# A gated group norm's scaling cut into two parts of two tiles, a weight tile apart

## The chip, the cores and the metric

The kernel runs on one core of one Trainium2 chip. The metric is the device time of one execution in microseconds (us). The kernel before took 1035.56 us (median of 3 runs, 1034.97 to 1035.7).

## The reference

Three transformer-like layers on 256 tokens of width 1024, in fp32. Layers 0 and 1 are a retention layer and a differential-attention layer, each with memory attention and a feed-forward part. Layer 2, which the change touches, has two mixers side by side, a state-space one (ssd, 16 heads) and a forgetting attention (fox, 16 heads). The end of the state-space mixer is a gated norm over two groups of 512 features:

```python
yg = (y * jax.nn.silu(z.astype(jnp.float32))).reshape(b, s, SSD_GROUPS, SSD_WIDTH // SSD_GROUPS)
yg = yg * lax.rsqrt(jnp.mean(yg * yg, axis=-1, keepdims=True) + NORM_EPS)
return (yg.reshape(b, s, SSD_WIDTH) * norm_w.astype(jnp.float32)).astype(xbc_raw.dtype)
```

Both mixers' outputs are then multiplied by the output weights and added to the stream x.

## The kernel before

Every large product runs with fp32 operands split into a high and a low part, three matmuls for each pair of 128x128 blocks. Weights stream through a ring of four slots. For each weight tile SyncE issues the load, ScalarE (ACT) copies the high part (`split_hi`, L1259), VectorE (DVE) subtracts to get the low part (`split_lo`, L1781), and TensorE (PE) multiplies (`project`). ACT and DVE split the tile that is four ahead of the one whose slot it takes. Two PSUM banks alternate in the input projection.

Layer 2's input projection `in2` has 45 weight tiles (slots 0 to 44); the first output projection `oa2` follows it (slots 45 to 52) and takes the eight state-space tiles as inputs, in order 0 to 7. Between the weight tiles the engines do the small work of the mixers. `plans()` writes by hand which step stands in which slot; each engine goes through the same list in program order and runs the steps that it has a part in, so an engine that waits in one step holds back all that stands behind it on that engine.

- PE runs the steps of a slot after that weight tile, except that `spread` and `ssd_out` come halfway through the next weight tile. From slot 20 on, tiles are taken in pairs with tokens on the partitions; the even slot's end completes a pair.
- DVE runs a slot in this order: early steps (`ssd_weights`, `norm_out`, then `ssd_skip` or `fox_probs`), the evacuation of the product (only even slots from 22 on), middle steps (`group_out`), `split_lo`, then late steps (`norm`, `ssd_gate`, `fox_values`, `fox_scores`, `head_sums`).
- ACT runs `split_hi`, then the slot's steps in plan order.
- GpSimd (POOL) runs its steps in plan order, without weight tiles: `ssd_mask` (L1729), `fox_bias` (L1738), `ssd_square` (L1721), `mix` (L1712).

The step of the change: `group_norm` (slot 29 for group 0, slot 40 for group 1) has PE form the mean of squares in bank 4 and ACT a first inverse root. `group_out` (slots 30 and 41) has DVE refine the root in three instructions (L1992, L1994, L2045) and scale the four 128x256 tiles of the group (L2049). The last one raises `np_out`. Then `mix` (slots 31 and 42) has ACT copy the high part of each of the four tiles (L1507) and POOL subtract to get the low part (L1712); `oa2` needs both (`mix_lo`).

`np_out` counts finished norms in order and has more readers. PE's `heads_turn` (the `spread` of the query and key norms, L1009) waits until all norms issued before it are out, since they use bank 4. ACT's `squares` (L1411) of norm n waits for norm n-2, whose buffer it takes over; the norm two behind group 0 is that of tiles 30 and 31 (`squares`, 30 in slot 31):

```python
if n >= 2:
    act.wait_ge(np_out, n - 1)
```

Around the change the plan has these steps (a selection). Slot 30: `group_out` 0, `ssd_square` 4, `ssd_weights` 5, `norm` 22. Slot 31: `ssd_skip` 5, `squares` 30, `spread` 22, `ssd_gate` 5, `ssd_decay` 12 and 13 (L1540), `fox_values` 0 (ACT L1563, then DVE L2202), `fox_scores` 1 (DVE L2189, then ACT L1550), `head_sums` 30, `mix` 0 to 3. Slot 32: `norm_out` 22 (L2031), `fox_probs` 1 (L2198, L1558), `ssd_square` 5, `ssd_out` 6 (L1189), `ssd_weights` 6 (L2164), `norm` 30, `fox_bias` 2. Slot 33: `ssd_skip` 6 (L2179), `spread` 30, `ssd_gate` 6 (L2209), `ssd_decay` 14 and 15, `fox_weights` 1 (L1106). Slot 34: `norm_out` 30, `ssd_weights` 7, `fox_scores` 2 (PE L1097). Slot 41: `group_out` 1, `fox_probs` 4, `head_sums` 26. Slot 42: `norm` 26, `mix` 4 to 7. Slot 43: `squares` 34, `spread` 26, `fox_values` 4, `fox_scores` 5. Slot 44: `norm_out` 26, `fox_probs` 5, `norm` 34, `fox_bias` 6. Slot 45: `spread` 34, `fox_weights` 5.

Of the kernel before, what the change touches and what calls it, by code (L numbers as in the profile page):

```python
# [24 lines left out]
T = 256  # L25
# [165 lines left out]
def plans():  # L191


    plan = {0: [[] for _ in range(28)], 1: [[] for _ in range(28)], 2: [[] for _ in range(61)]}

    def at(layer, slot, kind, *key):
        plan[layer][slot].append((kind, *key))
# [78 lines left out]
    for h, slots in enumerate(((9, 10, 11, 12), (11, 12, 13, 14), (13, 14, 15, 18), (15, 16, 17, 19),  # L276
                               (18, 19, 20, 21), (20, 21, 22, 23))):
        first, soft, turned, last = slots
# [44 lines left out]
    for j in range(4):  # L323
# [7 lines left out]
        for n in range(2):  # L331
            p, slot = 2 * j + n, a + 7 + 3 * n
# [6 lines left out]
        plan[2][21 + 2 * p].insert(0, ("ssd_skip", p))  # L339
    for g, slot in ((0, 29), (1, 40)):  # L340
        at(2, slot, "group_norm", g)
        plan[2][slot + 1].insert(0, ("group_out", g))
        for k in range(4):
            at(2, slot + 2, "mix", 4 * g + k)
    return plan


def program(nc, x_in, mem_in, params_in, consts_in, w, small_rows, out):
    f32, f32r = mybir.dt.float32, mybir.dt.float32r
    ALU, ACT = mybir.AluOpType, mybir.ActivationFunctionType  # L350
    AX = mybir.AxisListType.X
    PH, WIDTH = phases()
    PLAN = plans()
    NRING = len(WIDTH)
    MUL, ADD, SUB = ALU.mult, ALU.add, ALU.subtract
    ds = bass.ds

    with ExitStack() as ctx:
# [3 lines left out]
        def sem(name):  # L362
            return ctx.enter_context(nc.semaphore(name))
# [35 lines left out]
        def normed(n):  # L399
            return roots_b[:, :] if n % 2 else tmp[:, 1024:1536]  # L400
# [63 lines left out]
        np_sq, np_ms, np_ln, np_rt, np_nt, np_out = (sem(f"norm_{s}") for s in ("sq", "ms", "ln", "rt", "nt", "out"))  # L464
# [34 lines left out]
        def tile(buf, k, width=T):  # L499
            return buf[:, ds(k * T, width)]  # L500
# [4 lines left out]
        def pcol(name, k=0, rows=P):  # L505
            return par[0:rows, ds(k + PCOL[name], 1)]
# [19 lines left out]
        def eps(which, rows=P):  # L526
            return par[0:rows, PCOL["eps"] + which:PCOL["eps"] + which + 1]
# [60 lines left out]
        for layer in range(3):  # L588
            for steps in PLAN[layer]:
                for kind, *key in steps:  # L590
                    k = (layer, *key)
# [28 lines left out]
        def norm_bank(n):  # L620

            first = min(number["norm", k] for _, k in number if type(k[0]) is str and k[1] == 1 and _ == "norm")
            count_ = sum(1 for _, k in number if type(k[0]) is str and k[1] == 1 and _ == "norm")
            return bank[7 if 0 <= n - first < count_ and (n - first) % 2 else 4]
# [1141 lines left out]
        def _(dve):  # L1766
            V = nc.vector
# [219 lines left out]
            def newton_step(n, y, v=None):  # L1987


                dve.wait_ge(np_rt, n + 1)  # L1990
                v = norm_bank(n)[:, 0:y.shape[1]] if v is None else v
                V.scalar_tensor_tensor(v, v, eps(0), y, ADD, MUL).then_inc(np_nt, 1)  # L1992
                dve.wait_ge(np_nt, 5 * n + 1)
                V.tensor_tensor(v, v, y, MUL).then_inc(np_nt, 1)  # L1994
                dve.wait_ge(np_nt, 5 * n + 2)
                return v
# [41 lines left out]
                                                  norm_bank(norm_no(layer, t))[:, :], MUL, MUL)  # L2038
                last.then_inc(np_out, 1)

            def group_out(layer, g):
                n = number["norm", ("group_norm", layer, g)]
                y = normed(n)[:, 0:T]
                v = newton_step(n, y)
                V.scalar_tensor_tensor(y, v, -3.0, y, ADD, MUL).then_inc(np_nt, 3)  # L2045
                dve.wait_ge(np_nt, 5 * n + 5)
                for t in range(4 * g, 4 * g + 4):
                    y = tile(u, 8 + t)
                    last = V.scalar_tensor_tensor(y, y, pcol("ssdn", t), normed(n)[:, 0:T], MUL, MUL)  # L2049
                last.then_inc(np_out, 1)  # L2050

            def ret_scores(layer, h):
                dve.wait_ge(r_s, h + 1)
# [151 lines left out]
            def ssd_gate(layer, t):  # L2205
# [3 lines left out]
                V.tensor_tensor(y, y, tile(u, t), MUL).then_inc(ss_g, 1)  # L2209

            DO = {"head_sums": head_sums, "norm": norm, "norm_out": norm_out, "norm_soon": norm_out, "group_out": group_out, "ret_scores": ret_scores, "gated": gated, "gated_early": gated, "scores": scores,
                  "maxima_mid": scores, "softmax_mid": softmax, "norm_mid": norm_out, "mix_low": mix_low,
                  "mix_low_early": mix_low,
# [52 lines left out]
            for s in range(2):  # L2266
                last = V.tensor_tensor(lam[0:64, s:s + 1], par[0:64, lc + 2 * s:lc + 2 * s + 1],
                                       par[0:64, lc + 2 * s + 1:lc + 2 * s + 2], MUL)
# [134 lines left out]
```

## Time and profile before

| what | value |
|---|---|
| median of 3 runs | 1035.56 us |
| the profiled execution's own time | 1035.94 us |
| its span in the trace | 1034.0 us |
| TensorE busy | 1015.1 us, 98% |
| VectorE busy | 804.1 us, 78% |
| ScalarE busy | 635.6 us, 61% |
| GpSimd busy | 265.7 us, 26% |
| mean granted TensorE clock | 0.998 |

The span is the time from the first to the last instruction in the trace; the execution's own time holds 1.94 us more around it. The granted clock is a share of 2.4 GHz, so 0.50 is the lower level, 1.2 GHz. In the trace's rows an instruction has a start, a duration, its engine, its line in the kernel, what it writes and reads, and in brackets how long its engine stood idle before it and for whom.

### The profile page before, as it was taken

Reading aid. Unit: us, or ns where it says so; the run is one execution under the profiler, and the core shown is the slowest. Engines: PE = TensorE matmul, PEld = TensorE weight load, DVE = VectorE, ACT = ScalarE, POOL = GpSimd, SP = SyncE. Lnnn points to the kernel's source line nnn. Section 1 sums busy time; section 2 is a strip of 40 time slices with the busy share of each in tenths; the row PEclk is TensorE's granted clock in tenths of the full one; section 3 lists DMA queues with packets and bytes.
Section 4 is the critical chain, followed back from the end, with each engine's and each line's share of the span. In section 5 each row is a group of like instructions: output and inputs, shape, how many; then the busy total and the mean of one; then the engine's idle time right before and its main releaser. Section 6 shows DMA issues by size and latency. Waiting matters only on the chain.

```text
span 1034.0 us, 21367 instructions
## 1 busy us (share of the span) xinstructions
PE 1015.1 (98%) x7196; PEld 926.9 (90%) x7196; DVE 804.1 (78%) x1360; ACT 635.6 (61%) x1183; POOL 265.7 (26%) x236
## 2 busy tenths in 40 slices
PE   8999999999999999999999999999899999999998
PEld 7999988888889898888888899998798899999988
DVE  6875897877665988987787658979978689998843
ACT  7653786656554666765666446766776666666532
POOL 3200044544110000244453110035321034444300
PEclk9999999999999999999999999999999999999999
DMA  8543465565655332656555664565344455555663
GB/s 303 184 135 100 124 223 195 182 193 182 200 179 193 128 107 64 202 185 197 186 183 179 199 201 154 169 204 190 132 159 134 151 171 184 183 183 183 186 199 103
DMA packets 56898, 178.61 MB, mean 173 GB/s; under 512 B 6240, under 2 KB 11648, under 8 KB 56704
## 3 DMA queue, kind: packets, MB, share of 16 engines
q1 hardware_dynamic: 56832, 177.73, 53.5%
q8 instruction: 41, 0.67, 0.3%
q14 instruction: 25, 0.20, 0.1%
HBM read 176.63 MB, written 1.08 MB: 172 GB/s over the span
## 4 chain that ended last, share of the span: by engine, by line
PE 52%; DVE 6%; ACT 3%; issue 1%; DMA 1%; DVEq 0%; SPq 0%; ACTq 0%
PE bank L822 7%; PE bank L820 5%; PE bank L821 5%; PE bank L818 4%; PE bank L816 4%; PE scores L822 4%; PE scores L816 4%; PE scores L818 4%; PE scores L820 2%; PE scores L821 2%; PE bank L815 2%; PE scores L815 2%; DVE ring_parts L1781 1%; PE bank L848 1%; PE bank L849 1%
## 5 line engine op out<-in xcount | busy, mean ns | idle before, releaser
L1781 DVE TENSOR_TENSOR ring_parts<-ring_raw,ring_parts 128x1024 fp32r<-128x1024 f32 (+2 forms) x343 | 423.1, 1236 | 34.4 <-ACT ring_parts L1259 28.8
L1259 ACT ACTIVATE ring_parts<-ring_raw 128x1024 fp32r<-128x1024 f32 (+2 forms) x343 | 340.9, 997 | 73.9 <-PE scores L816 31.1
L822 PE MATMUL bank<-xw_parts,ring_parts 128*128 128x256 f32 x648 | 182.3, 281 | 0.0
L820 PE MATMUL bank<-xw_parts,ring_parts 128*128 128x256 f32 x472 | 136.4, 289 | 0.2 <-DVE con L1932 0.2
L821 PE MATMUL bank<-xw_parts,ring_parts 128*128 128x256 f32 x472 | 133.5, 283 | 0.0
L822 PEld LDWEIGHTS bank<-xw_parts,ring_parts 128*128 128x128 f32 x648 | 123.4, 190 | 7.5
L848 PE MATMUL bank<-ring_parts,xw_parts 128*128 128x256 f32 x384 | 114.3, 298 | 0.2 <-DVE u L1975 0.2
L849 PE MATMUL bank<-ring_parts,xw_parts 128*128 128x256 f32 x384 | 108.9, 284 | 0.0
L850 PE MATMUL bank<-ring_parts,xw_parts 128*128 128x256 f32 x384 | 108.9, 284 | 0.0
L1679 POOL TENSOR_TENSOR act_parts<-tmp,act_parts 128x256 f32 (+1 forms) x66 | 61.6, 933 | 166.4 <-ACT act_parts L1335 166.4
L822 PE MATMUL scores<-xw_parts,ring_parts 128*128 128x256 f32 x352 | 98.6, 280 | 0.0
L822 PE MATMUL bank<-act_parts,ring_parts 128*128 128x256 f32 x337 | 94.5, 281 | 0.0
L820 PEld LDWEIGHTS bank<-xw_parts,ring_parts 128*128 128x128 f32 x472 | 90.3, 191 | 2.2 <-issue 1.3
L821 PEld LDWEIGHTS bank<-xw_parts,ring_parts 128*128 128x128 f32 x472 | 90.4, 191 | 0.1
L848 PEld LDWEIGHTS bank<-ring_parts,xw_parts 128*128 128x128 f32 x384 | 73.7, 192 | 7.4 <-issue 6.9
L1675 POOL TENSOR_TENSOR scratch<-scratch 128x256 f32<-128x256 f32 x47 | 46.5, 989 | 119.6 <-ACT scratch L1270 118.2
L1687 POOL TENSOR_TENSOR tmp<-tmp,rstd 128x256 f32<-128x256 f32 x44 | 74.1, 1684 | 9.4 <-ACT tmp L1340 9.2
L849 PEld LDWEIGHTS bank<-ring_parts,xw_parts 128*128 128x128 f32 x384 | 73.8, 192 | 0.1
L850 PEld LDWEIGHTS bank<-ring_parts,xw_parts 128*128 128x128 f32 x384 | 73.7, 192 | 0.0
L822 PEld LDWEIGHTS scores<-xw_parts,ring_parts 128*128 128x128 f32 x352 | 66.9, 190 | 7.5
L1340 ACT ACTIVATE tmp<-tmp 128x256 f32<-128x256 f32 x66 | 27.6, 419 | 70.7 <-DVE tmp L1941 41.9
L818 PE MATMUL scores<-xw_parts,ring_parts 128*128 128x512 f32 x176 | 70.0, 398 | 0.5 <-DVE xw_parts L1787 0.5
(267 smaller groups left out, 2594.3 us busy)
## 6 DMA issues: line engine op xcount, KB each, us to landing
ring_raw<-w_up SPq DMA_DIRECT2D x132, 512.0 KB, 3.5
ring_raw<-w_in SPq DMA_DIRECT2D x85, 512.0 KB, 3.6
ring_raw<-w_down SPq DMA_DIRECT2D x48, 512.0 KB, 3.7
ring_raw<-w_down SPq DMA_DIRECT2D x24, 384.0 KB, 4.0
ring_raw<-w_oa SPq DMA_DIRECT2D x16, 256.0 KB, 2.6
ring_raw<-w_ob SPq DMA_DIRECT2D x16, 256.0 KB, 2.9
ring_raw<-w_oa SPq DMA_DIRECT2D x8, 512.0 KB, 3.5
ring_raw<-w_ob SPq DMA_DIRECT2D x8, 512.0 KB, 3.6
```

Of the source, the lines that this page charges most:

```text
L816: return mm(ps[:, 0:2 * T], w_hi, tile(parts, 2 * t, 2 * T), start=False, stop=stop)
L818: mm(ps[:, 0:2 * T], w_hi, tile(parts, 2 * t, 2 * T), start=start, stop=False)
L820: mm(ps[:, 0:T], w_hi, high(parts, t), start=start, stop=False)
L821: mm(ps[:, 0:T], w_hi, low(parts, t), start=False, stop=False)
L822: return mm(ps[:, 0:T], w_lo, high(parts, t), start=False, stop=stop)
L848: mm(o, x_hi, w_hi, start=not second and k == 0 and tt == 0, stop=False)
L849: mm(o, x_hi, w_lo, start=False, stop=False)
L850: last = mm(o, x_lo, w_hi, start=False, stop=second and k == 3 and tt == 1)
L1259: A(ring_hi[:, slot * DM:slot * DM + width], ring_raw[:, slot * DM:slot * DM + width], ACT.Copy).then_inc(hi_done, 1)
L1679: G.tensor_tensor(low(act_parts, f), two(prod, h), high(act_parts, f).bitcast(f32), SUB).then_inc(ffn_lo, 1)
L1687: G.tensor_tensor(two(gate_s, h), two(gate_s, h), rstd[:, :], MUL).then_inc(silu_scaled, 1)
L1781: V.tensor_tensor(ring_lo[:, a:b], ring_raw[:, a:b], ring_hi[:, a:b].bitcast(f32), SUB).then_inc(lo_done, 1)
```

## The change

`group_out` gets a third key, the part. Part 0 (slots 30 and 41) refines the root and scales the first two tiles; part 1 (slots 31 and 42) scales the other two and raises `np_out`. The four `mix` steps of each group move from slots 31 and 42 to slots 32 and 43, at the end of each slot's list.

```diff
@@ plans()
     for g, slot in ((0, 29), (1, 40)):
         at(2, slot, "group_norm", g)
-        plan[2][slot + 1].insert(0, ("group_out", g))
+        for part in range(2):
+            plan[2][slot + 1 + part].insert(0, ("group_out", g, part))
         for k in range(4):
-            at(2, slot + 2, "mix", 4 * g + k)
+            at(2, slot + 3, "mix", 4 * g + k)
     return plan
@@ vector engine
-            def group_out(layer, g):
+            def group_out(layer, g, part):
+
                 n = number["norm", ("group_norm", layer, g)]
-                y = normed(n)[:, 0:T]
-                v = newton_step(n, y)
-                V.scalar_tensor_tensor(y, v, -3.0, y, ADD, MUL).then_inc(np_nt, 3)
-                dve.wait_ge(np_nt, 5 * n + 5)
-                for t in range(4 * g, 4 * g + 4):
+                if part == 0:
+                    y = normed(n)[:, 0:T]
+                    v = newton_step(n, y)
+                    V.scalar_tensor_tensor(y, v, -3.0, y, ADD, MUL).then_inc(np_nt, 3)
+                    dve.wait_ge(np_nt, 5 * n + 5)
+                for t in range(4 * g + 2 * part, 4 * g + 2 * part + 2):
                     y = tile(u, 8 + t)
                     last = V.scalar_tensor_tensor(y, y, pcol("ssdn", t), normed(n)[:, 0:T], MUL, MUL)
-                last.then_inc(np_out, 1)
+                if part:
+                    last.then_inc(np_out, 1)
```

## Rows read from the trace of the kernel before

**Rows 1.** The page's busy time of each engine: time, share of the span, instructions
```profile
PE 1015.1 (98%) x7196; PEld 926.9 (90%) x7196; DVE 804.1 (78%) x1360; ACT 635.6 (61%) x1183; POOL 265.7 (26%) x236
```
**Rows 2.** Stretches, us: busy time (instructions) of PE, PEld, DVE, ACT, POOL; PEclk; DMA
```profile
739.40:743.00 3.60, 3.60 (x20) 3.60 (x19) 3.07 (x3) 3.57 (x10) 3.60 (x5) 0.53 0.24 61
...
790.00:800.00 10.00, 8.64 (x60) 6.78 (x59) 8.85 (x19) 6.38 (x16) 0.00 (x0) 1.00 0.42 145
```
**Rows 3.** PE's waits, 690 to 800 us: total, times, longest
```profile
PE bank L1189 <- DVE tmp L2164: 1.9, 1, 1.9
PE scores L1097 <- DVE u L2031: 1.8, 2, 1.3
PE bank L1009 <- DVE u L2013: 1.4, 3, 0.6
PE scores L1106 <- ACT tmp L1558: 1.4, 1, 1.4
```
**Rows 4.** DVE's timeline, slots 30 to 32: start, duration, instruction, idle before it
```profile
727.44 2.64 DVE L2049 SCALAR_TENSOR_TENSOR u<-u,par,tmp 128x256 f32<-128x256 f32 x4
730.00 1.21 DVE L1781 TENSOR_TENSOR ring_parts<-ring_raw,ring_parts 128x1024 fp32r<-128x1024 f32 x1
...
732.86 1.22 DVE L1781 TENSOR_TENSOR ring_parts<-ring_raw,ring_parts 128x1024 fp32r<-128x1024 f32 x1
...
734.33 0.42 DVE L2202 TENSOR_TENSOR act_parts<-bank,act_parts 128x256 fp32r<-128x256 f32 x1
...
737.03 0.95 DVE L2164 TENSOR_TENSOR tmp<-tmp,u 128x768 f32<-128x768 f32 x1
...
739.40 1.63 DVE L1781 TENSOR_TENSOR ring_parts<-ring_raw,ring_parts 128x1024 fp32r<-128x1024 f32 x1 [0.76 <-ACT ring_parts L1259]
741.52 0.81 DVE L1992 SCALAR_TENSOR_TENSOR heads<-heads,par 128x8 f32<-128x8 f32 x1 [0.49 <-ACT heads L1416]
```
**Rows 5.** ACT's timeline, slots 31 and 32
```profile
730.17 0.63 ACT L1411 ACTIVATE tmp<-u 128x512 f32<-128x512 f32 x1 [1.57 <-DVE u L2049]
730.71 1.48 ACT L1540 ACTIVATE tmp<-tmp 128x256 f32<-128x256 f32 x4
732.10 0.36 ACT L1563 ACTIVATE act_parts<-bank 128x256 fp32r<-128x256 f32 x1
...
737.10 1.32 ACT L1507 ACTIVATE act_parts<-u 128x256 fp32r<-128x256 f32 x4
```
**Rows 6.** PE's timeline, slots 31 to 34
```profile
732.61 0.66 PE L1009 MATMUL bank<-con,u 128*128 128x128 f32 x4
...
738.03 0.87 PE L1189 MATMUL bank<-tmp,x_tok 128*64 128x256 f32 x8 [1.91 <-DVE tmp L2164]
...
744.59 0.66 PE L1009 MATMUL bank<-con,u 128*128 128x128 f32 x4 [0.41 <-DVE u L2013]
...
747.98 0.38 PE L1097 MATMUL scores<-u 64*128 64x128 f32 x2 [0.50 <-DVE u L2031]
```
**Rows 7.** POOL's mixes: timeline, then the line L1712's min, median, max in ns
```profile
737.58 4.04 POOL L1712 TENSOR_TENSOR act_parts<-u,act_parts 128x256 fp32r<-128x256 f32 x4 [8.18 <-ACT act_parts L1507]
L1712 POOL TENSOR_TENSOR act_parts<-u,act_parts x8: 722/730/1704, 737.6 to 785.4; 128x256 fp32r<-128x256 f32 x8
```
**Rows 8.** DVE's small norm step L1992: count, min, median, max ns
```profile
L1992 DVE SCALAR_TENSOR_TENSOR heads<-heads,par x8: 215/228/809, 702.5 to 793.4; 128x8 f32<-128x8 f32 x8
```
**Rows 9.** Timelines of DVE, ACT and PE around slots 42 to 45
```profile
783.40 0.69 DVE L1992 SCALAR_TENSOR_TENSOR heads<-heads,par 128x8 f32<-128x8 f32 x1
...
788.75 0.40 ACT L1550 ACTIVATE tmp<-tmp,negmax 128x128 f32<-128x128 f32 x1 [3.46 <-DVE negmax L2189]
...
786.75 0.66 PE L1009 MATMUL bank<-con,u 128*128 128x128 f32 x4 [0.56 <-DVE u L2013]
788.67 0.40 PE L818 MATMUL bank<-act_parts,ring_parts 128*128 128x512 f32 x1
...
793.00 0.88 PE L1106 MATMUL scores<-con,tmp 128*128 128x128 f32 x6 [1.35 <-ACT tmp L1558]
```

## The prediction

> **What bounds the kernel now.** I read the page's busy times first: PE is busy for 1015.1 us of a span of 1034.0 [rows 1]. So nothing that this change does can matter unless it moves one of PE's idle spells or the clock that PE gets. The work of PE is not changed. Next I read PE's waits in the stretch that the change touches, slots 23 to 48, 690 to 800 us [rows 3]. There are seven, together 6.5 us: one on `ssd_weights` (1.9), two on `norm_out` (1.8), three on the token-wise norms (1.4), one on ACT's attention weights (1.4). All but the last are on DVE. Of them the change can reach five: 1.91 us at 738.03, 0.41 at 744.59, 0.50 at 747.98 [rows 6], 0.56 at 786.75 and 1.35 at 793.00 [rows 9], sum 4.7. Then the clock: in 739.40 to 743.00 PE was granted 0.53 of full speed, so nearly all the time at the lower level, 1.2 GHz [rows 2]. What PE did before that was to stand idle for 1.91 us. The dip costs (1 - 0.53) x 3.6 = 1.7 us. So 4.7 + 1.7 = 6.4 us is all that the change could win here, were every wait gone.
>
> Between 727 and 738 DVE has work at almost every moment, and PE waits for the end of that queue: the row of `ssd_weights` 6 starts at 737.03, and PE's `ssd_out` 6 at 738.03 [rows 4, 6]. `group_out` lies in that queue.
>
> **Group 0, part 0 (slot 30).** The change takes two of four L2049 out of slot 30. The four took 2.64 us from 727.44 [rows 4], so 0.66 each. But they are put back in slot 31 ahead of `split_lo`, and between the two places DVE waits for nobody: the split at 730.00, the norm of 22, `ssd_skip` 5 and the split at 732.86 follow each other at once. So the whole of `group_out` is now over where the split of slot 31 starts today, at about 732.9 instead of 730.1, and everything from that split on starts when it did. Gain on DVE's queue: nothing. The split and the norm between are some 0.8 to 1.3 us earlier, and nobody waits for them except PE's L1009 at 732.61 [rows 6], which from now on has to wait for `np_out` (bank 4) as well, until about 732.9. That puts PE's arrival at `ssd_out` 6 off by 0.3 us, and it would find the queue not finished anyway. Cost nothing here.
>
> **Group 0, the wait of ACT (slot 31).** This is the term that I think is real. ACT's `squares` 30 takes over the group norm's buffer and waits for `np_out`; it stood idle 1.57 us for L2049 already and began at 730.17 [rows 5]. It can now begin at about 732.95, 2.8 us later. Queued behind it on ACT are `ssd_decay` 12 and 13 (1.48) and the copy of `fox_values` 0, which began at 732.10 and ended at 732.46, 2.3 us after the squares began [rows 5]. So that copy ends at 732.95 + 2.3 = 735.25. DVE wants it for L2202, at 734.33 [rows 4]. DVE stalls 735.3 - 734.33 = 0.95 us, and `fox_scores` 1, `head_sums` 30, `norm_out` 22 and `ssd_weights` 6 behind it are late by as much. `ssd_out` 6 starts at 739.0 instead of 738.03, and PE's idle spell is 1.91 + 0.95 - 0.3 = about 2.6 us. **+0.95 us** on PE's time at that point. The clock falls as before; I take the dip at its present 1.7 us.
>
> **Group 0, the mixes (slot 31 to 32).** The four L1507 took 1.32 us of ACT ahead of `split_hi` of slot 32 [rows 5], and DVE's split at 739.40 had waited 0.76 us for that one [rows 4]. With ACT's exponentials 0.95 us late and the mixes gone from there, `split_hi` comes at 738.2 to 739.2, and DVE, which reaches its split at 739.6, doesn't wait. The norm of 30 (741.52, after a wait of 0.49 for ACT [rows 4]) comes 0.2 us earlier. So DVE has made good its delay there. Then the mixes come, behind the norm on ACT at about 741.3 to 742.6, ahead of `split_hi` of slot 33, and on POOL behind `ssd_square` 5 and `fox_bias` 2, at about 743 to 747. Today POOL's four mixes take 737.58 to 741.62 [rows 7], where DVE has idle gaps. While POOL works, DVE's instructions with both inputs in SBUF are stretched: the split at 739.40 took 1.63 against 1.21, L1992 0.81 against a median of 0.228 [rows 4, 8], and one mix took 1.704 against 0.730 [rows 7]. In the new place DVE has the norm's multiply, a split, `ssd_gate` 6 and `ssd_weights` 7. I bound what that adds before `norm_out` 30, for which PE waits at 747.98 [rows 6]: below, nothing (the stretching only moves); above, four times the 0.42 us of the split, 1.7 us, less the 0.2 that DVE is ahead, so +1.5. I take 0.7, since POOL's total is the same and only the place is worse.
>
> The Trainium skill, "SBUF — State Buffer", section "SBUF: two separate sides", says that a GpSimd instruction and a DVE instruction with two SBUF inputs lock each other out for the whole of an instruction. By it each of the four mixes could hold up one DVE instruction for its whole 0.73 us, at most 2.9 us in all, and then PE's time after 748 would be about 2.2 us later than mine; the trace agrees that such instructions alternate, in the stretched rows of [rows 4, 7, 8], though less than whole lengths were lost.
>
> **Sum of group 0 at 748 us.** PE is 0.95 late at 738. The waits of 0.41 and 0.50 [rows 6] absorb 0.91 of it, if DVE is on time for them; DVE is 0 to 1.5 late, 0.5 with my value (0.7 - 0.2). PE leaves 747.98 at +0.5; bounds 0.05 and 1.5. After it PE has no wait until 786, so that stays.
>
> **Group 1.** Two L2049 leave slot 41 and come back in slot 42, before its split. `norm` 26 starts at 783.40 as before, but POOL is now silent, so its three small instructions take about 0.2 each instead of 0.69 [rows 8, 9], 1.4 less, and I put another 0.4 on L2013. PE's wait of 0.56 at 786.75 goes: **-0.56**. DVE is then 1.8 us ahead, and ACT's exponentials of `fox_scores` 5 start at 788.75 - 1.8 = 786.9 [rows 9]. Behind them come the mixes (slot 43), ACT 788.7 to 790.0, POOL from 789.1. At 0.73 each without contention, the low parts of tiles 4 to 7 are there at 789.85, 790.6, 791.3 and 792.0; with one of them 1.7 long, the last at 793.0. Here is what is late next: `oa2` began at 788.67 and was through its first tile 1.35 before 793.00, at 791.65 [rows 9], 0.37 us for each of eight blocks. It now begins at 788.1, so it wants input 4 at 789.6 and input 7 at 790.7. It will stand idle at every one of them and end at 792.4 to 793.4, not 791.1. Behind it PE's L1106 started at 793.00 after a wait of 1.35 for ACT [rows 9]; ACT would be ready at 792.4. So PE starts L1106 at 792.4 to 793.4 against 793.00: **-0.6 to +0.4**, I take 0 (the middle, rounded toward contention). The wait of 1.35 is replaced by the wait for the mixes.
>
> **The sum** against the profiled execution's own 1035.94 us: +0.5 + 0 = 1036.4. That execution was 0.38 above the median of the runs, so against the median it is 1035.56 + 0.5 = **1036.1 us**. A measurement of this kernel can tell about 0.2%, 2.1 us, from no change, so this is "no change".
>
> **Rivals.** (a) POOL against DVE decides: the mixes of group 0 stretch all four DVE instructions, the bound of +1.5 comes true and group 1 ends at +0.4: +1.9, **1037.5 us**. For it: [rows 8]; against it: it only decides if POOL's mixes fall fully between 743 and 747. It is still within the 0.2%. (b) Slower: the clock falls a second time. Its place is `oa2`'s first tile, 789.5 to 793.4, where PE would idle 1.5 to 2.5 us in pieces; its price is the measured 1.7 us of the first dip, on top of +0.5 and +0.4: +2.6, **1038.2 us**. It decides once PE's idle share there is that of 736 to 738, where 1.91 us was followed by a fall; 1.35 us at 791.6 was not, PEclk is 1.00 in 790 to 800 [rows 2, 6, 9]. The same price falls due if the longer idle spell at 738 prolongs the dip. (c) Faster: the ACT wait is absorbed and DVE gets through earlier, because its small norm steps no longer collide with POOL (3 x 0.5 us in each group). Then the waits at 738 (to below 1.5 us), 744.59, 747.98 and 786.75 shrink by 0.5 + 0.41 + 0.50 + 0.56 = 2.0, and without the long idle spell the clock stays up: -1.7. Together -3.7, **1031.9 us**. Against it: `squares` 30 waits for the last L2049 [rows 5], and no DVE work before 737 becomes less. (d) The change does nothing, since the two parts lie in the same unbroken DVE queue and all waits only trade places: 0, 1035.6. It is one end of my own case.
>
> **How the numbers follow.** My case with (d) at its lower end: 0.60. (a) 0.18. (b) 0.13. (c) 0.09. Within 0.2%: 0.60 + 0.18 = 0.78, and a little of (b) and (c) falls short of the limit, so 0.80; slower 0.12; faster 0.08. The range takes in the bounds of my case (-0.6 to +1.9), half a us of spread between runs, and part of (b): 1034.5 to 1038.1.
>
> **What would show it.** In the profile after: L1411 with a longer idle before it (about 4.3 us, 1.57 before), L2202 in slot 31 with an idle near 0.95 for ACT's L1563, PE's L1189 with 2.6 instead of 1.91. No idle before the split of slot 32. The wait at 786.75 gone. PE idle on POOL's L1712 before four products of `oa2`. A PEclk near 0.5 only once, after 739. I am wrong if L2202 has no wait, if the clock doesn't dip after 738, or if it dips near 793 as well.

## The result, and the profile after

The changed kernel took 1037.44 us, the kernel before, timed beside it, 1035.70 us (medians of 19 runs each). The ratio is 1.0017, 95% interval 1.0011 to 1.0023: slower by 1.7 us, within the 0.2% that the prediction called "no change", but clear of zero. The profiled execution took 1037.02 us, with a span of 1035.1.

PE's waits from 690 to 800 us, as in [rows 3]: total, times, longest.

```profile
PE bank L1190 <- DVE tmp L2168: 2.5, 1, 2.5
PE scores L1098 <- DVE u L2032: 2.5, 2, 1.3
PE bank L816 <- POOL act_parts L1713: 1.1, 1, 1.1
PE bank L1010 <- DVE u L2052: 0.6, 1, 0.6
PE bank L1010 <- DVE u L2014: 0.4, 1, 0.4
PE bank L819 <- POOL act_parts L1713: 0.4, 1, 0.4
```

Lines have moved: most by 1, `ssd_weights` from L2164 to L2168, the norm's scaling L2049 to L2052. Three waits are new, of two kinds: one for the last L2052 (bank 4), two for POOL's mixes. The wait for ACT's attention weights before L1106 is gone.

All of the loss arises between three starts on PE that every trace has: `fox_scores` 1 (716.56 before, 716.29 after), `fox_scores` 2 (747.98 and 748.83), and `fox_weights` 5 (793.00 and 794.27). The first stretch went from 31.42 to 32.54 us, **+1.12**; the second from 45.02 to 45.44, **+0.42**. Together +1.54, against +1.7 in the medians (the two profiled executions are only 1.08 apart, since the changed one was 0.27 ahead at 716 us and 0.2 quicker after the second stretch). I use these two stretches for every kernel below, since what happens before 716 us differs from execution to execution by several tenths. A stretch comes from one trace. In traces of programs that are the same up to there it repeats within 0.1 us (31.36 to 31.47, 32.53 to 32.63), with one exception of 0.23 that is explained below.

First stretch, ACT in slot 31, then DVE in slots 31 to 34 (as [rows 5] and [rows 4]):

```profile
732.83 0.63 ACT L1412 ACTIVATE tmp<-u 128x512 f32<-128x512 f32 x1 [4.49 <-DVE u L2052]
733.36 1.48 ACT L1541 ACTIVATE tmp<-tmp 128x256 f32<-128x256 f32 x4
734.75 0.36 ACT L1564 ACTIVATE act_parts<-bank 128x256 fp32r<-128x256 f32 x1
```

```profile
732.65 1.22 DVE L1782 TENSOR_TENSOR ring_parts<-ring_raw,ring_parts 128x1024 fp32r<-128x1024 f32 x1
...
735.15 0.42 DVE L2206 TENSOR_TENSOR act_parts<-bank,act_parts 128x256 fp32r<-128x256 f32 x1 [0.94 <-ACT act_parts L1564]
...
739.38 1.22 DVE L1782 TENSOR_TENSOR ring_parts<-ring_raw,ring_parts 128x1024 fp32r<-128x1024 f32 x1
741.18 0.36 DVE L1993 SCALAR_TENSOR_TENSOR heads<-heads,par 128x8 f32<-128x8 f32 x1 [0.59 <-ACT heads L1417]
...
743.03 1.11 DVE L2014 TENSOR_TENSOR u<-u,heads 128x512 f32<-128x512 f32 x1
744.07 0.47 DVE L2183 SCALAR_TENSOR_TENSOR u<-u,par,bank 128x256 f32<-128x256 f32 x1
744.46 1.36 DVE L1782 TENSOR_TENSOR ring_parts<-ring_raw,ring_parts 128x1024 fp32r<-128x1024 f32 x1
745.75 0.95 DVE L2213 TENSOR_TENSOR u<-u 128x256 f32<-128x256 f32 x1
746.63 1.48 DVE L2168 TENSOR_TENSOR con<-con,u 128x768 f32<-128x768 f32 x1
748.03 0.74 DVE L2032 TENSOR_SCALAR u<-bank,par 128x512 f32<-128x512 f32 x1
```

ACT stood idle for 4.49 us where it had 1.57, and passed it on to DVE as an idle of 0.94 in front of L2206. The split at 739.38 now waits for nobody (0.76 before). But the next lines are stretched: L2014 1.11 against 0.69 without POOL, the split 1.36 against 1.22, L2213 0.95 against 0.42, L2168 1.48 against 0.95. Sum 1.62 us. Counted from `fox_scores` 1 in both kernels, DVE is 1.09 us late at L2168 (`ssd_weights` 6). When L2014 starts, at 743.03, it has made that good and is 0.54 ahead (L2013 started at 743.84 before). At L2032 it is 1.12 late (L2031, 747.18 before), and that is the whole loss of the stretch. The trace of the kernel before has the same multiply once beside POOL's mixes of group 1, and as long:

```profile
785.58 1.12 DVE L2013 TENSOR_TENSOR u<-u,heads 128x512 f32<-128x512 f32 x1
```

POOL's rows in the changed kernel say why; the second is group 1:

```profile
742.86 4.44 POOL L1713 TENSOR_TENSOR act_parts<-u,act_parts 128x256 fp32r<-128x256 f32 x4
...
789.98 3.78 POOL L1713 TENSOR_TENSOR act_parts<-u,act_parts 128x256 fp32r<-128x256 f32 x4 [14.17 <-ACT act_parts L1508]
```

PE's rows over both stretches (as [rows 6, 9]):

```profile
732.88 0.63 PE L1010 MATMUL bank<-con,u 128*128 128x128 f32 x4 [0.55 <-DVE u L2052]
...
738.86 0.87 PE L1190 MATMUL bank<-tmp,x_tok 128*64 128x256 f32 x8 [2.48 <-DVE tmp L2168]
...
748.83 0.93 PE L1098 MATMUL scores<-u 64*128 64x128 f32 x8 [1.17 <-DVE u L2032]
...
790.76 0.50 PE L819 MATMUL bank<-act_parts,ring_parts 128*128 128x512 f32 x1 [0.44 <-POOL act_parts L1713]
...
793.81 0.39 PE L816 MATMUL bank<-act_parts,ring_parts 128*128 128x256 f32 x1 [1.05 <-POOL act_parts L1713]
...
794.27 0.81 PE L1107 MATMUL scores<-con,tmp 128*128 128x128 f32 x6
```

And the clock, the last but two of the columns, here 0.66 and 1.00: one fall, after 738, none at the first output tile.

```profile
740.00:745.00 5.00, 5.00 (x32) 5.00 (x31) 4.24 (x7) 4.97 (x16) 4.20 (x6) 0.66 0.29 105
790.00:795.00 5.00, 3.36 (x17) 2.01 (x17) 3.07 (x5) 4.71 (x12) 5.00 (x6) 1.00 0.17 51
```

### The profile page after: what moved, and what is told of

Read it like the earlier page. It is cut to its first block, busy times and chain, and to the rows that moved or that the text cites. A ratio compares the mean times of both kernels' runs of the same rounds, so it can differ in the third digit from the quotient of the medians.

```text
span 1035.1 us, 21367 instructions
## 1 busy us (share of the span) xinstructions
PE 1016.6 (98%) x7196; PEld 928.3 (90%) x7196; DVE 804.0 (78%) x1360; ACT 635.7 (61%) x1183; POOL 265.9 (26%) x236
## 3 DMA queue, kind: packets, MB, share of 16 engines
HBM read 176.63 MB, written 1.08 MB: 172 GB/s over the span
## 4 chain that ended last, share of the span: by engine, by line
PE 52%; DVE 6%; ACT 3%; issue 1%; POOL 0%; DVEq 0%; ACTq 0%
PE bank L823 7%; PE bank L821 5%; PE bank L822 5%; PE bank L819 4%; PE bank L817 4%; PE scores L823 4%; PE scores L819 4%; PE scores L817 4%; PE scores L821 2%; PE scores L822 2%; PE bank L816 2%; PE scores L816 2%; DVE ring_parts L1782 2%; PE bank L849 1%; PE bank L850 1%
## 5 line engine op out<-in xcount | busy, mean ns | idle before, releaser
L819 PE MATMUL bank<-xw_parts,ring_parts 128*128 128x512 f32 x176 | 69.7, 396 | 0.8 <-DVE xw_parts L1788 0.8
```

The source lines that it names most:

```text
L819: mm(ps[:, 0:2 * T], w_hi, tile(parts, 2 * t, 2 * T), start=start, stop=False)
```

## The experiments

All experiments are in this table, but for two more profiles of the kernel with the mixes moved alone, which come at the end. "Stretch 1" is from PE's `fox_scores` 1 to 2, "stretch 2" on to `fox_weights` 5, from one trace; the ratios are to the kernel before, timed beside it (medians of 11 runs, before of 27 to 33). A ratio is estimated together with its interval and can differ from the quotient of the two medians by up to 0.0005. An interval is about 0.9 us to either side, so the medians tell apart only the largest differences, and most of what follows rests on the stretches.

| kernel | stretch 1 | stretch 2 | median us | before | ratio, interval |
|---|---|---|---|---|---|
| before | 31.42 | 45.02 | | | |
| changed (19 runs) | 32.54 | 45.44 | 1037.44 | 1035.70 | 1.0017 (1.0011 to 1.0023) |
| mixes moved alone | 31.42 | 45.44 | 1037.58 | 1035.86 | 1.0016 (1.0007 to 1.0025) |
| split alone | 32.30 | 45.03 | 1036.64 | 1035.86 | 1.0008 (0.9999 to 1.0017) |
| group 0 alone | 32.53 | 45.00 | 1037.29 | 1035.86 | 1.0015 (1.0006 to 1.0024) |
| group 1 alone | 31.19 | 45.41 | 1036.59 | 1035.86 | 1.0012 (1.0003 to 1.0022) |
| changed, squares behind | 31.51 | 46.92 | 1036.71 | 1035.92 | 1.0012 (1.0002 to 1.0021) |
| changed, mixes 0 late | 31.29 | 45.43 | 1036.71 | 1035.92 | 1.0005 (0.9996 to 1.0014) |
| changed, mixes 1 first | 32.63 | 45.03 | 1036.86 | 1035.92 | 1.0009 (1.0000 to 1.0018) |
| before, mixes 0 late | 30.19 | 45.03 | 1034.74 | 1035.92 | 0.9987 (0.9978 to 0.9996) |
| the same, weights first | 29.86 | 45.03 | 1034.46 | 1035.92 | 0.9986 (0.9977 to 0.9995) |
| changed, all three mended | 29.88 | 45.02 | 1034.30 | 1035.92 | 0.9986 (0.9977 to 0.9995) |

**Which half of the change costs?** Mixes moved, `group_out` whole:

```diff
-            at(2, slot + 2, "mix", 4 * g + k)
+            at(2, slot + 3, "mix", 4 * g + k)
```

> Only the mix steps move a slot later; group_out stays whole. Theory (two terms: ACT's squares of 30 wait 2.8 us longer because of the split, and POOL's mixes stretch VectorE's instructions in a worse place): without the split, PE's idle spell before ssd_out 6 stays at 1.9 us, the squares' idle stays near 1.6, but the mixes still hit VectorE in slots 33 and 34, so PE's wait before scores 2 is about 1.2 to 2 us against 0.5, and group 1 ends 0.4 us late: +1.0 to +1.5 us over the kernel before. Rival (the split makes the whole loss): 0 to +0.3 us.

Stretch 1 is 31.42, exactly as before: in group 0 the new place is no worse than the old one. The part of the theory that gave it +0.6 to +1.1 fell. Stretch 2 is +0.42, as expected. DVE's rows show how the zero comes about:

```profile
737.85 1.21 DVE L1781 TENSOR_TENSOR ring_parts<-ring_raw,ring_parts 128x1024 fp32r<-128x1024 f32 x1
739.65 0.37 DVE L1992 SCALAR_TENSOR_TENSOR heads<-heads,par 128x8 f32<-128x8 f32 x1 [0.59 <-ACT heads L1416]
...
741.50 1.11 DVE L2013 TENSOR_TENSOR u<-u,heads 128x512 f32<-128x512 f32 x1
```

The idle of 0.76 before the split is gone, the split is 0.42 shorter and L1992 0.44 (1.63 and 0.81 in [rows 4]), together 1.62. The four instructions from L2013 on are stretched by as much again. The median doesn't follow the stretches: it is +1.7 us, as much as for the whole change and 1.3 more than they explain. The profiled execution was this kernel's fastest, at 1035.36 us. I come back to that.

**The split alone**, on the changed kernel:

```diff
-            at(2, slot + 3, "mix", 4 * g + k)
+            at(2, slot + 2, "mix", 4 * g + k)
```

> Only the split of group_out; the mixes stay in slots 31 and 42. Theory: squares of 30 idle 4.5 us, PE idle 2.5 us before ssd_out 6, but no mixes in slots 33 and 34, so about 0 to +0.9 us from group 0, and group 1 near 0: +0.3 to +0.9 us. Rival (the mixes' place is the whole loss): 0. Rival (the split makes the whole loss): +1.7 us.

Stretch 1 is +0.88, stretch 2 unchanged, the median +0.8, within what the theory had. DVE in that trace:

```profile
735.92 0.42 DVE L2206 TENSOR_TENSOR act_parts<-bank,act_parts 128x256 fp32r<-128x256 f32 x1 [0.94 <-ACT act_parts L1564]
...
740.99 1.63 DVE L1782 TENSOR_TENSOR ring_parts<-ring_raw,ring_parts 128x1024 fp32r<-128x1024 f32 x1 [0.76 <-ACT ring_parts L1260]
...
746.20 1.21 DVE L1782 TENSOR_TENSOR ring_parts<-ring_raw,ring_parts 128x1024 fp32r<-128x1024 f32 x1
```

The 0.94 us is there, the old idle of 0.76 and the old stretched split of 1.63 too. So 0.94 of delay comes in, and 0.88 arrives at `fox_scores` 2: with the mixes in their old place DVE makes up next to nothing.

**One group at a time.** The key `part` and the moved mixes for one group only; the other has both parts in one slot and its mixes where they were:

```diff
-        for part in range(2):
-            plan[2][slot + 1 + part].insert(0, ("group_out", g, part))
+        for part in (0, 1) if g == 0 else (1, 0):
+            plan[2][slot + 1 + (part if g == 0 else 0)].insert(0, ("group_out", g, part))
-            at(2, slot + 3, "mix", 4 * g + k)
+            at(2, slot + (3 if g == 0 else 2), "mix", 4 * g + k)
```

> The whole change for group 0 only. Theory: +1.1 us, all of it there by PE's scores 2 near 749 us; the stretch after 780 us as in the kernel before. Rival (group 1's mixes, late for the output projection, make most of the loss): under +0.4 us.

+1.11 in stretch 1 and nothing in stretch 2, as the theory had it; the median is +1.4.

The same with `g == 1`:

> The whole change for group 1 only. Theory: PE's wait before the norm transposes at 786.8 (0.56 us) goes, waits of together 1.5 us for POOL's mixes come in the first tile of the output projection, the wait of 1.35 us for ACT goes: +0.4 us in sum. Rival (group 1 makes most): +1.2 us or more.

+0.39 in stretch 2 (45.41). The wait of 1.35 for ACT is gone, POOL's 0.44 and 1.05 are there. By the ratios group 1 seems to cost as much as group 0, but the intervals overlap widely; of its 11 runs seven lie between 1035.87 and 1036.65, four between 1037.49 and 1038.66. I come back to that.

This kernel's stretch 1 is that of the kernel before in its program, and its trace shows something about the clock. First the stretches 730 to 750, then PE's rows:

```profile
730.00:740.00 10.00, 8.10 (x69) 6.87 (x66) 9.07 (x24) 6.71 (x21) 2.19 (x3) 1.00 0.41 132
740.00:750.00 10.00, 7.97 (x67) 6.72 (x65) 9.20 (x13) 6.93 (x17) 4.41 (x6) 1.00 0.42 133
```

```profile
738.26 0.87 PE L1190 MATMUL bank<-tmp,x_tok 128*64 128x256 f32 x8 [1.90 <-DVE tmp L2168]
741.04 0.87 PE L1107 MATMUL scores<-con,tmp 128*128 128x128 f32 x6 [0.28 <-ACT tmp L1559]
744.59 0.66 PE L1010 MATMUL bank<-con,u 128*128 128x128 f32 x4 [1.24 <-DVE u L2014]
747.98 0.93 PE L1098 MATMUL scores<-u 64*128 64x128 f32 x8 [0.51 <-DVE u L2032]
```

The idle spell is the same 1.90 us, and the clock did not fall. Yet stretch 1 is only 0.23 us shorter. From `ssd_out` 6 to `fox_scores` 2 PE's own time was 1.35 us shorter than in the kernel before, and its waits were 1.12 longer: 0.28 for ACT, 1.24 and 0.51 for DVE, instead of 0.41 and 0.50, both for DVE. The 0.23 that is left is on DVE's side too, where the small norm step (L1993, 0.23 us) was not stretched as in the kernel before (0.81) and L2014 was (1.10 for 0.69). So of the 1.7 us that I had charged to the fall [rows 2] nearly all was hidden. In this kernel DVE's queue binds the stretch, whatever PE's clock does.

**Is it what stands behind the waiting squares?** The changed kernel, with this added:

```diff
+    plan[2][31].remove(("squares", 30))
+    plan[2][31].insert(plan[2][31].index(("fox_values", 0)) + 1, ("squares", 30))
```

> The changed kernel, but in slot 31 ACT's squares of tiles 30 and 31 come behind ssd_decay 12, 13 and fox_values 0 instead of ahead of them. Theory (the split costs group 0 its time through what stands behind the waiting squares on ACT): VectorE's wait of 0.94 us for ACT's copy of fox_values 0 goes, PE's idle spell before ssd_out 6 is back at 1.6 to 1.9 us, and PE gets to scores 2 0.7 to 1.1 us earlier; -0.7 to -1.1 us against the changed kernel, so about +0.8 against the kernel before. Rival (VectorE is late by POOL's mixes alone): PE's scores 2 stay where they are, +1.7 against the kernel before.

DVE's idle before its `fox_values` 0 is gone, PE's idle spell is 1.44 (1.6 to 1.9 expected), stretch 1 is 31.51, 1.03 shorter than in the changed kernel. The rival fell. Stretch 2 of this execution was 46.92, though, 1.5 longer than its like, and that is the clock: PE's rows, then 749 to 750.

```profile
738.36 0.87 PE L1192 MATMUL bank<-tmp,x_tok 128*64 128x256 f32 x8 [1.44 <-DVE tmp L2170]
743.74 0.66 PE L1012 MATMUL bank<-con,u 128*128 128x128 f32 x4 [0.80 <-DVE u L2016]
748.35 1.12 PE L1100 MATMUL scores<-u 64*128 64x128 f32 x8 [1.73 <-DVE u L2034]
```

```profile
749.00:750.00 1.00, 1.00 (x7) 0.60 (x4) 1.00 (x1) 1.00 (x3) 0.06 (x1) 0.50 0.10 26
```

Here the clock stayed up after 1.44 us of idling and fell to 1.2 GHz after 1.73, at about 749. The lower clock, from 749 to nearly 753, takes away 1.7 us of full speed, and stretch 2 is 1.5 longer, so next to nothing is hidden here. Five of this kernel's 11 runs took 1037.87 to 1039.35 us, six 1035.82 to 1036.71. Each run's mean granted clock goes with that: 1.000, so no fall anywhere, in five of the six short ones, 0.996 to 0.998 in all five long ones. Its median says little, the stretch says much.

**Is it the mixes that keep DVE from catching up?** The changed kernel, with group 0's mixes in slot 39, where ACT, POOL and DVE all have gaps:

```diff
-            at(2, slot + 3, "mix", 4 * g + k)
+            at(2, 39 if g == 0 else slot + 3, "mix", 4 * g + k)
```

> The changed kernel, with group 0's mixes in slot 39 instead of 32. Theory (ACT's wait is the root, the mixes keep VectorE from catching up): idle of 2.5 us before ssd_out 6 stays, but VectorE's instructions of slots 33 and 34 are no longer stretched (split 1.2, gate 0.4, ssd_weights 7 0.95), and PE's wait before scores 2 falls from 1.17 us to under 0.3: -0.9 to -1.1 us against the changed kernel, +0.6 to +0.8 against the kernel before. Rival (the mixes' place does nothing): +1.7. In both, part of the executions is 1.7 us longer by a second fall of the clock in the first output tile.

PE still idles for 2.48 us before `ssd_out` 6, and then waits for nothing:

```profile
739.63 0.87 PE L1190 MATMUL bank<-tmp,x_tok 128*64 128x256 f32 x8 [2.48 <-DVE tmp L2168]
...
748.36 0.93 PE L1098 MATMUL scores<-u 64*128 64x128 f32 x8
```

Stretch 1 is 31.29, 1.25 shorter than in the changed kernel, and the median is +0.8, as expected. So either cost can be taken away, and each time about a microsecond comes back.

**The same move on the kernel before:**

```diff
-            at(2, slot + 2, "mix", 4 * g + k)
+            at(2, 39 if g == 0 else slot + 2, "mix", 4 * g + k)
```

> The kernel before, with group 0's mixes in slot 39 instead of 31. Theory (until scores 2 at 748 us VectorE is the bound, and POOL's and ACT's mixes in slots 31 and 32 lengthen its queue): the split of slot 32 waits no more for ACT and isn't stretched, PE's waits of 0.41 and 0.50 us before the transposes and scores 2 go: -0.9 us. Rival (PE is the bound, by its idle spell of 1.9 us and the fall of the clock after it): 0.

Stretch 1 is 30.19, -1.23; the median 1.2 us under the kernel before (-0.9 expected). DVE's rows of slots 32 to 34 show the splits and the four instructions that the changed kernel stretches at their plain length. The small norm steps are still stretched, now beside `ssd_square` 5 and `fox_bias` 2. POOL's mixes in slot 39 take 2.83 us instead of 4.04:

```profile
738.35 1.22 DVE L1781 TENSOR_TENSOR ring_parts<-ring_raw,ring_parts 128x1024 fp32r<-128x1024 f32 x1
740.15 0.37 DVE L1992 SCALAR_TENSOR_TENSOR heads<-heads,par 128x8 f32<-128x8 f32 x1 [0.59 <-ACT heads L1416]
740.55 0.66 DVE L1994 TENSOR_TENSOR heads<-heads 128x8 f32<-128x8 f32 x1
...
742.01 0.69 DVE L2013 TENSOR_TENSOR u<-u,heads 128x512 f32<-128x512 f32 x1
...
743.01 1.22 DVE L1781 TENSOR_TENSOR ring_parts<-ring_raw,ring_parts 128x1024 fp32r<-128x1024 f32 x1
744.14 0.42 DVE L2209 TENSOR_TENSOR u<-u 128x256 f32<-128x256 f32 x1
744.48 0.95 DVE L2164 TENSOR_TENSOR con<-con,u 128x768 f32<-128x768 f32 x1
```

```profile
767.56 2.83 POOL L1712 TENSOR_TENSOR act_parts<-u,act_parts 128x256 fp32r<-128x256 f32 x4 [5.45 <-ACT act_parts L1507]
```

DVE reaches `norm_out` 30 (L2031) 1.63 us earlier than in the kernel before, counted from `fox_scores` 1, and PE then doesn't wait for it. The clock fell after 738 in this execution, so now it is PE that binds, and only 1.23 of the 1.63 arrive.

**One step further**, in slot 32 `ssd_weights` 6 ahead of `norm_out` 22 on DVE:

```diff
-                        planned = sorted(planned, key=lambda step: step[0] in last)
+                        planned = sorted(planned, key=lambda step: (step[0] in last, step[0] != "ssd_weights"))
```

> The kernel before with group 0's mixes in slot 39, and in slot 32 VectorE does ssd_weights 6 ahead of norm_out 22. Theory (with the mixes away PE's own time binds up to scores 2, by 0.5 us over VectorE's): PE's idle spell before ssd_out 6 falls from 1.90 us to 1.25, PE reaches scores 2 0.5 us earlier, and a fall of the clock there, if any, is paid only as far as PE doesn't wait for VectorE: -1.7 us against the kernel before, -0.5 against the variant with the mixes moved alone. Rival (VectorE still binds): as that variant, -1.2.

```profile
737.30 0.87 PE L1189 MATMUL bank<-tmp,x_tok 128*64 128x256 f32 x8 [1.24 <-DVE tmp L2164]
...
742.91 0.66 PE L1009 MATMUL bank<-con,u 128*128 128x128 f32 x4 [1.03 <-DVE u L2013]
...
746.30 0.93 PE L1097 MATMUL scores<-u 64*128 64x128 f32 x8 [0.51 <-DVE u L2031]
```

The idle spell is 1.24 us, as expected, and the clock stayed up. Stretch 1 is 29.86, only 0.33 less than without this step (0.5 expected): DVE binds again, with waits of 1.03 and 0.51. In the times the two variants can't be told apart (1.5 us under the kernel before, 1.7 expected).

**Group 1's mixes ahead of `fox_scores` 5.** The changed kernel, the mixes at the head of slot 43:

```diff
+    ahead = [step for step in plan[2][43] if step[0] == "mix"]
+    plan[2][43] = ahead + [step for step in plan[2][43] if step[0] != "mix"]
```

> The changed kernel, with group 1's mixes at the head of slot 43 instead of its end. Theory (the mixes of group 1 are late for the output projection because they stand behind ACT's wait for fox_scores 5, and PE's idle in pieces lets the clock fall in part of the executions): PE's waits for POOL's L1713 (1.5 us) go, the wait for ACT before fox_weights 5 comes back in part, no execution has the extra 1.7 us: the spread between runs shrinks from 2.2 us to about 1.2, and the median is +0.9 to +1.3 over the kernel before instead of +1.7. Rival (the place within the slot does nothing): +1.7 with the same spread.

PE's waits for POOL are gone, those of 0.56 and 1.35 us [rows 9] are back, stretch 2 is 45.03 as before. The median is +0.9 us; the runs spread over 1.6 us against 2.2, not over the 1.2 that was expected.

**All three mended:** squares behind `fox_values` 0, group 0's mixes in slot 39, group 1's at the head of slot 43, on the changed kernel.

> The changed kernel with all three suspected costs taken away: squares of 30 behind fox_values 0, group 0's mixes in slot 39, group 1's mixes at the head of slot 43. Theory (these three are the whole loss, and the split in itself brings and costs nothing): as the kernel before with its mixes in slot 39, -1.0 to -1.3 us against the kernel before, and no slow executions. Rival (the split has a cost of its own, by PE's wait for np_out before the norm transposes of slot 31): -0.3 or worse.

Stretches 29.88 and 45.02; -1.6 us in the medians, a little more than the theory had, and all 11 runs within 1 us. The rival fell: no cost of the split itself shows. No clear gain does either. It ends where the variant of the kernel before with weights first ends. Compared with the plain move of the mixes (30.19), it has 0.31 less in this one trace; in that other trace PE's clock had fallen after 738 and here it had not, and DVE comes to `norm_out` 30 0.09 us later here, so the 0.31 can't be given to the split.

**The spread.** The runs of the five kernels with group 1's mixes in slot 43 behind `fox_scores` 5 spread over 2.0 to 3.5 us each, those of the six others over 0.9 to 1.6. The kernel with only the mixes moved spread over 3.2 us, so it was profiled twice more.

> The kernel with only the mix steps moved, looked at once more, because its times spread over 3.2 us and its first trace was of the fastest execution. Theory (PE's idle in pieces at the first output tile, together with the waits before it, lets the clock fall a second time in most executions): in an execution over 1037.2 us the clock is at half speed for 3.4 us somewhere between 790 and 800 us, which adds 1.3 to 1.7 us. Rival: the clock stays up there and the added time lies elsewhere.

> A last look at the kernel with only the mix steps moved. Both traces of it so far were of executions under 1037 us and had the clock up around the first output tile. Theory (second fall of the clock in most executions): if this execution is over 1037.2 us, its trace shows the half-speed clock for about 3.4 us near 791 to 797 us and PE reaches fox_weights 5 or the tiles behind it 1.3 to 1.7 us later. Rival: an execution over 1037.2 us with the clock up there, the time lost elsewhere. An execution under 1037 us tells neither.

The second time it took 1037.49 us (median of 8 runs, ratio 1.0014, interval 1.0004 to 1.0024), the third time there was one run, of 1036.33. Neither profiled execution was over 1037.2 us (1036.63 and 1036.33); in both the clock stayed up around the first output tile, and their stretches are 31.47 and 31.36, 45.44 and 45.42. Of its 20 runs in all, 13 took 1037.2 us or more, while the stretches explain +0.42. So a second fall of the clock is **not shown** at that tile. It was seen once, in the kernel with the squares behind, at 749 us. The mean granted clock of each run is the only further trace of it. In the changed kernel the four runs at 0.995 or 0.996 are the four slowest (1038.0 to 1038.92 us), and the 15 at 0.997 or more took 1036.76 to 1037.79. One fall of the measured size takes 0.0016 off that mean. But the mean doesn't say where a fall stood. Some traces, that of the changed kernel among them, have one between 0 and 20 us, outside both stretches, and with only the mixes moved runs at 0.998 took anything from 1035.36 to 1038.51 us. What adds the last microsecond to those runs stays open.

## Why the prediction was right, and where it was off

The time came out at 1037.44, in the range (1034.5 to 1038.1), with "no change" at 0.2% as forecast, but 1.3 us over the point. That class says little, since the prediction's own case, rival (a) and rival (d) all lay in it. The likeliest case gave way to rival (a), which had 1037.5 and whose condition was met: POOL's mixes ran from 742.86 to 747.30. That the two numbers meet so closely is in part luck: (a) had +1.9 us where the traces show +1.54, and the kernel before came out at 1035.70 this time, not 1035.56.

- **Part 0 brings nothing.** Right. The split of slot 31 started at 732.65 behind the second part, and PE's L1010 waited 0.55 us for it, without consequence: the kernel with all three mended has this wait too. The 0.66 us for each L2049 was not their plain length, though. POOL's `ssd_mask` ran beside them; alone two of them take 0.87. In the changed kernel it is the split of slot 30 that stands beside it, 1.75 us long instead of 1.21.
- **ACT's wait, +0.95.** Right: DVE's new idle is 0.94, PE's idle spell 2.48 against the 2.6 forecast. What it passed on was 1.09 us on DVE and 1.10 on PE at `ssd_out` 6, counted from `fox_scores` 1. The kernel with the squares moved behind shows it to be the cause, 1.03 us of stretch 1.
- **"So DVE has made good its delay there."** Right, and too careful: the split no longer waits, and at the norm's multiply (L2014) DVE was 0.54 us ahead, not 0.2. But see the next point.
- **"I take 0.7, since POOL's total is the same and only the place is worse."** This is the step that failed. The four instructions were stretched by 1.62 us, nearly the upper bound of 1.7, though not the 2.9 us that the whole lengths of four mixes would have cost. The trace of before showed L1992 under POOL's load, at 0.81 for 0.228 [rows 8], and the norm's multiply itself, 1.12 us long beside group 1's mixes. For group 1 the prediction took these 0.4 us into its sum, for group 0 it didn't. Group 0 so came to 1.66 lost and 0.54 ahead, +1.12, between my +0.5 and the bound of +1.5.
- **Group 1, 0 within -0.6 to +0.4.** The mechanism was right in each part: the wait of 0.56 gone, POOL's mixes late, the wait for ACT replaced. Only the waits for POOL are two (0.44 and 1.05 us), not one at each of the four inputs. The sum came at the upper end, +0.42: with 0.85 us taken off, by which `fox_scores` 2 is later now, POOL began at 789.13, where I had it (789.1), and its four mixes took 3.78 us, close to the 3.9 of the contended case. The middle that I took was again too kind to POOL.
- **The clock's 1.7 us as part of what could be won.** Wrong for the fall after 738: where the clock stayed up, PE waited longer for DVE, and 0.23 us came of it. The group 1 kernel shows it. Rival (c) counted on the full 1.7, so its -3.7 was too much even on its own terms.
- **Rival (b)**, a second fall, has one trace for it, elsewhere than forecast and in another kernel, and the mean clocks of the slowest runs of the changed kernel, which don't say where.

The Trainium skill, "TensorE: Matmul & The Clock Gate", section on the HAM clock gate, says that the monitor runs free of the kernel's start, so that one and the same kernel can see its clock change at another point. The traces agree: after the same 1.90 us of idling before `ssd_out` 6 the clock fell in one execution (mixes moved alone) and stayed up in another (group 1 alone).

**What the change was up against.** In group 0 neither half wins anything. The split delays ACT's squares, and by them DVE, by about a microsecond. Moving the mixes frees DVE from one idle of 0.76, one stretched split (0.42) and one stretched L1992 (0.44), and stretches four others by 1.62 in exchange: nothing in sum. Where they are neither here nor there but in slot 39, the kernel before gains 1.2 us, and the changed kernel, with its other two costs mended, 1.6.

## What to carry to other kernels

When a step is cut in two, ask which semaphore its last instruction raises and what stands behind each engine that waits for it: here a buffer's hand-over on a third engine, with an unrelated copy queued behind it, turned a cut that cost nothing on its own engine into almost a microsecond. GpSimd work is worth placing where VectorE is idle or reads PSUM; beside VectorE's SBUF-to-SBUF work the four mixes cost it 1.62 us here, about 0.4 each, and where it was idle or read PSUM they took 2.83 us instead of 4.44. A fall of the clock cost 0.23 us at most where TensorE waited for VectorE behind it, and 1.5 where it didn't; before counting one as something to win, look for the wait that would take its place.

## What the runs showed of the hardware

- A VectorE instruction on 128x8 elements with both inputs in SBUF took mostly 0.59 to 0.81 us beside POOL's 128x256 instructions, and 0.17 to 0.23 alone. What is lost is not a share of the length: a 128x256 and a 128x768 instruction lost 0.53 us each, a 128x512 one 0.42, the 128x1024 split between 0.14 (1.36) and 0.55 (1.77 in the group 0 kernel). An instruction that read PSUM in the midst of the mixes (L2183 at 744.07) took its usual 0.47.
- POOL's four 128x256 subtractions took 2.83 us while VectorE was idle or read PSUM, and 3.27 to 4.44 beside its work in SBUF.
- The clock fell after idle spells of 1.73, 1.90 and 2.48 us, and in other executions stayed up after 1.24, 1.44 and 1.90.
